# A hybrid MLA and sliding-window decoder step on one core: weight rings, the values' weights and the sums of squares between the two layers

## The reference

```python
for i in range(DEPTH):
    ap = rmsnorm(hp, pre_norm[i])
    ...
        mp = gated_out(o.reshape(n_b, seq, MLA_WIDTH), gate, mla_w_o[l])      # i = 0
        ...
        q, k, v, gate = swa_project(ap, swa_w_in[l])                          # i = 1
    ...
    hp = hp + rmsnorm(mp, post_norm[i])
```

## Time and profile before

| | |
|---|---|
| median of 3 runs | 1773.57 us (1772.23 to 1782.35) |
| the profiled execution | 1772.12 us |
| its span, first to last instruction | 1770.4 us |
| mean granted clock of TensorE | 0.963 |
| PE busy | 1628.7 us, 92% |
| DVE busy | 820.6 us, 46% |
| ACT busy | 545.9 us, 31% |
| POOL busy | 733.1 us, 41% |

### The profile page before, as it was taken

One profiled execution on the slowest core, in us unless ns is written; L12 is line 12 of the kernel. 1 busy time (PEld: TensorE's weight loads), 2 busy tenths in 40 slices (PEclk: granted clock), 3 DMA queues, 4 the chain that ended last, 5 costly groups with the idle time before them and its releaser, 6 DMA issues. The chain is left out here.

```text
span 1770.4 us, 28128 instructions
## 1 busy us (share of the span) xinstructions
PE 1628.7 (92%) x10778; PEld 1521.7 (86%) x10778; DVE 820.6 (46%) x1474; ACT 545.9 (31%) x1201; POOL 733.1 (41%) x891
## 2 busy tenths in 40 slices
PE   6999997899999999999988879997999899799797
PEld 6989997799989999998986569997899899576697
DVE  5127311676575766657563310038543201587016
ACT  5022111344444444444432210022222201576012
POOL 2323332255554555555445214545233222487410
PEclk9999998999999999999999989998999999799698
DMA  4112231111121111121149872252543122542214
GB/s 169 60 48 95 95 113 64 36 61 51 63 66 52 57 63 64 57 66 57 40 157 309 315 286 73 71 191 96 189 158 134 38 86 107 156 120 72 82 48 160
DMA packets 101406, 186.92 MB, mean 106 GB/s; under 512 B 11058, under 2 KB 65091, under 8 KB 100995
## 3 DMA queue, kind: packets, MB, share of 16 engines
q1 hardware_dynamic: 86628, 139.36, 23.6%
q0 software_dynamic: 8448, 24.65, 4.0%
q10 hardware_dynamic: 6208, 21.26, 3.0%
HBM read 137.42 MB, written 49.89 MB: 106 GB/s over the span
## 5 line engine op out<-in xcount | busy, mean ns | idle before, releaser
L607 POOL TENSOR_SCALAR b_prob<-b_prob,b_share 128x896 f32<-128x896 f32 (+7 forms) x128 | 97.1, 760 | 198.5 <-DVE b_share L806 196.7
L1607 POOL CAST w_hi_d<-w_raw_d 128x1024 fp32r<-128x1024 f32 x50 | 55.9, 1118 | 289.8 <-PE ps L129 114.7
L129 PE MATMUL ps<-a_xh,w_hi_a 128*128 128x344 f32 x552 | 119.6, 325 | 13.7 <-DVE a_xl L280 10.5
L707 ACT ACTIVATE b_pth<-ps 128x512 fp32r<-128x512 f32 (+1 forms) x160 | 86.2, 555 | 104.3 <-PE ps L930 94.7
L129 PE MATMUL ps<-a_xl,w_hi_a 128*128 128x344 f32 x552 | 118.2, 323 | 0.0
L129 PE MATMUL ps<-a_xh,w_lo_a 128*128 128x344 f32 x552 | 117.3, 321 | 0.0
L797 DVE TENSOR_REDUCE b_least<-ps 128x1 f32<-128x896 f32 (+7 forms) x128 | 96.3, 752 | 35.6 <-PE ps L916 34.9
L698 ACT ACTIVATE b_prob<-ps,b_least 128x896 f32<-128x896 f32 (+7 forms) x128 | 94.9, 744 | 57.1 <-DVE b_least L797 56.2
L811 DVE TENSOR_TENSOR b_ptl<-ps,b_pth 128x512 fp32r<-128x512 f32 (+1 forms) x160 | 99.2, 633 | 27.1 <-ACT b_pth L707 26.1
L1869 PE MATMUL ps<-xo_h,w_hi_d 128*128 128x344 f32 x352 | 98.3, 331 | 13.7 <-DVE w_lo_d L1747 7.1
L1610 POOL TENSOR_TENSOR w_lo_d<-w_raw_d,w_hi_d 128x1024 fp32r<-128x1024 f32 x42 | 106.2, 2529 | 3.4
(11 more groups left out here) (324 smaller groups left out, 4618.4 us busy)
## 6 DMA issues: line engine op xcount, KB each, us to landing
w_raw_d<-in_w_tiles SPq DMA_DIRECT2D x52, 512.0 KB, 3.6
c_pages<-in_cache_pages SPq DMA_DIRECT2D x80, 160.0 KB, 4.4
w_raw_a<-in_w_tiles SPq DMA_DIRECT2D x23, 512.0 KB, 3.5
gate_scratch<-a_stage ACTq DMA_DIRECT2D x16, 512.0 KB, 2.6
b_gate<-gate_scratch SPq DMA_DIRECT2D x64, 128.0 KB, 2.5
oh_scratch<-b_oh POOLq DMA_DIRECT2D x64, 128.0 KB, 2.1
ol_scratch<-b_ol POOLq DMA_DIRECT2D x64, 128.0 KB, 2.1
xo_h<-oh_scratch SPq DMA_DIRECT2D x16, 512.0 KB, 10.6
```

What stands on the lines that cost most here:

```text
L129: mm = nc.tensor.matmul(ps[:, bank + c, 0:CH], wt, xt[:, k0 + k, c * CH:(c + 1) * CH], start=first and x == 0, stop=last and x == 2)
L607: nc.gpsimd.tensor_scalar(prob[:, n % 4, 0:keys], prob[:, n % 4, 0:keys], share[:, n % 4:n % 4 + 1], 1.0, ALU.mult, ALU.mult).then_inc(nor ...
L707: nc.scalar.activation(pth[:, n % 4, 0:cols], ps[:, 4 + n % 2, 0:cols], ACT.Copy).then_inc(pt_hi, 1)
L1607: nc.gpsimd.tensor_copy(w.hi[:, t % 2, :], w.raw[:, t % 2, :]).then_inc(w.rounded, 1)
```

## The change

It edits only the stretch between the layers, `mla_samples` and `out_and_swa_front`.

- **Samples.** The products with `xo_l` of heads 0 to 7 now stand ahead of the transpose; those of heads 0 and 1 with `xo_h` follow; then tile 1's low part and heads 8 to 15 of `xo_l`. `LOW_PARTS` are four groups of four heads.
- **Raw ring.** Six tiles of the second pass (20, 21, 24, 25, 28, 29) are loaded into two more places, `raw_more`. So a load waits for the split of the tile four before; tiles 20 and 21 wait only for `totals`.
- **High and low ring.** In the second pass it has three places; the third is 8 blocks of 128 columns each for high and low inside `xo_l`, columns that the first pass has used. `parts`, `parts_of` and `shaped` give the views.
- **Values.** Tiles 42 and 43 have high and low places of their own, `wv_hi` and `wv_lo`, and wait for the stores of h (`h_out`). Tiles 44 and 45 follow the use of tiles 40 and 41 in the ring.
- **DVE's order.** The remainders of tiles 23, 25 and 27 stand ahead of a step each; the sums of the late squares 2 to 4 are spread anew. `sum_late`, `diag_early` and some other small tiles move; the late squares have three places instead of four.
- **Sums of h's late squares.** POOL adds squares 0 to 3 (three additions, behind the split of tile 33), DVE adds 4 to 7 (three) and then both sums (one).
- **PE.** The replication of the late inverse roots stands ahead of the product group k = 4 instead of behind it.
- **Sinks.** DVE negates them behind the first two queries.

The diff, cut to its core:

```diff
-LOW_PARTS = (range(0, 5), range(5, 9), range(9, 13), range(13, 16))
+LOW_PARTS = (range(0, 4), range(4, 8), range(8, 12), range(12, 16))
...
         mm.then_inc(cols_made, 1)
-        pe.wait_ge(w.split, 2)
-        part(1, range(KT), range(2), w.lo, g.xo_h)
+        low(0, False)
+        low(1, False)
         pe.wait_ge(cols_kept, 1)
...
         pe.wait_ge(xo_first_in, 32)
         part(0, range(2), range(2), w.hi, g.xo_h)
-        part(0, range(2), range(2), w.lo, g.xo_h)
-        for i, heads_in in enumerate(LOW_PARTS):
...
+        part(0, range(2), range(2), w.lo, g.xo_h).then_inc(w.used, 1)
+        pe.wait_ge(w.split, 2)
+        part(1, range(KT), range(2), w.lo, g.xo_h)
+        low(2, False)
+        low(3, True).then_inc(w.used, 1)
...
+    third = xo_l[:, 0:KT, CH:CH + P], xo_l[:, 0:KT, CH + P:CH + 2 * P]
+    raw_more = at("m_raw_more", [P, 2, D], 156672)
+    wv_hi, wv_lo = at("f_wv_hi", [P, 2, D], 200064, R32), at("f_wv_lo", [P, 2, D], 191808, R32)
...
+    v_tiles = (first_f + NQ + NKV - 2, first_f + NQ + NKV - 1)
+    raw_slot = [2 + t % 2 if t in (20, 21, 24, 25, 28, 29) else t % 2 for t in range(n_tiles)]
+    raw_before = [max((b for b in range(t) if raw_slot[b] == raw_slot[t]), default=None) for t in range(n_tiles)]
+    slot = [(t - N_OUT + 2) % 3 if N_OUT <= t < first_f else t % 2 for t in range(n_tiles)]
+    slot_before = [max((b for b in range(t) if slot[b] == slot[t] and b not in v_tiles), default=None) for t in range(n_tiles)]
...
-            split_done(sp, t - 2)
-            nc.sync.dma_start(w.raw[:, t % 2, :], a["w_tiles"][tile]).then_inc(w.landed[t % 2], 16)
+            sp.wait_ge(totals, 1) if raw_before[t] is None else split_done(sp, raw_before[t])
+            nc.sync.dma_start(raw_tile(t), a["w_tiles"][tile]).then_inc(landed[raw_slot[t]], 16)
...
+            if t in v_tiles:
+                pool.wait_ge(h_out, 32 * KT)
+            else:
+                pool.wait_ge(w.used, max((slot_before[t] or 0) + 1, N_OUT - 1 if slot[t] == 2 else 0))
...
+        for t in range(2, first_f + 2):
+            split(t)
+        for k in range(1, 4):
+            pool.wait_ge(h_sq, KT + k + 1)
...
+            nc.gpsimd.tensor_tensor(h_sum[:, SPLIT:TOK], h_sq_late[:, 0, :] if k == 1 else h_sum[:, SPLIT:TOK],
+                                    h_sq_late[:, k, :], ALU.add).then_inc(h_added_pool, 1)
+        for t in range(first_f + 2, n_tiles):
+            split(t)
...
-        for k in range(1, KT):
-            add_square(1, k)
+        for k in range(5, KT):
+            add_square_late(k)
+        dve.wait_ge(h_added, KT + 2)
+        dve.wait_ge(h_added_pool, 3)
+        nc.vector.tensor_tensor(h_sum[:, SPLIT:TOK], h_sum[:, SPLIT:TOK], h_sq_late[:, 4, :], ALU.add).then_inc(h_added, 1)
...
-                wh, wl = w.hi[:, half, k * P:(k + 1) * P], w.lo[:, half, k * P:(k + 1) * P]
+                wh, wl = parts_of(t, k)
...
-        for k in range(2, 5):
+        for k in range(2, 4):
             part(0, k, (0, 1))
         pe.wait_ge(spaced, 2)
         pe.wait_ge(unit, KT)
         replicate(diag_late, 0, 7)
+        part(0, 4, (0, 1))
         part(0, 5, (0, 1))
...
-                for x, (xt, wt) in enumerate(((g.xh, w.hi), (g.xh, w.lo), (g.xl, w.hi))):
+                for x, (xt, wt) in enumerate(((g.xh, wv_hi), (g.xh, wv_lo), (g.xl, wv_hi))):
```

More of the change, by code:

```diff
@@ L1423, in tensor, with low @@
         mm.then_inc(cols_made, 1)
-        pe.wait_ge(w.split, 2)
-        part(1, range(KT), range(2), w.lo, g.xo_h)
+        def low(i, last):
+            pe.wait_ge(xo_low_in[i], 16 * len(LOW_PARTS[i]))
+            for h in LOW_PARTS[i]:
+                mm = part(h // KT, range(h % KT, h % KT + 1), range(2), w.hi, xo_l, last=last and h == H - 1)
+            return mm
+        low(0, False)
+        low(1, False)
         pe.wait_ge(cols_kept, 1)
@@ L1782, in vector, with add_square_late @@
+        def add_square_late(k):
+            dve.wait_ge(h_sq, KT + k + 1)
+            if k > 5:
+                dve.wait_ge(h_added, KT + k - 6)
+            nc.vector.tensor_tensor(h_sq_late[:, 4, :], h_sq_late[:, 4, :], h_sq_late[:, k, :], ALU.add).then_inc(h_added, 1)
         for j in range(1, KT):
             add_early(j)
-        rest(N_OUT + 1)
+        rest(17)
         spaces(of_early, diag_early, 6, rooted, 1, inverted, spaced)
-        rest(N_OUT + 3)
+        rest(19)
         dve.wait_ge(replicated, 2)
@@ L1807, in vector @@
+        rest(27)
+        to_unit(0, 6), add_x(0, 6), x_low(0, 5), add_square(5), add_late(3)
+        to_unit(0, 7), add_x(0, 7), x_low(0, 6), add_square(6)
+        rest(29)
+        x_low(0, 7), add_square(7), add_late(4)
+        add_late(5)
+        rest(31)
+        add_late(6)
+        add_late(7)
         spaces(of_late, diag_late, 3, rooted, 2, inverted, spaced)
@@ L1810, in vector @@
         dve.wait_ge(read_late, KT)
[L1811 to L1812 removed]
+        to_unit(1, 0), add_x(1, 0)
         for k in range(1, KT):
@@ L1843, in vector @@
         scale(0), scale(1), query_low(0), query_low(1)
+        dve.wait_ge(sinks_in, 16)
+        nc.vector.tensor_scalar(g.nsinks[:], g.sinks[:], -1.0, None, ALU.mult).then_inc(negated, 1)
         for j in range(2, NQ):
```

104 lines of the change are left out of this document (52 added, 52 removed).

## The result

| | before | after |
|---|---|---|
| median | 1776.78 us (9 runs, 1772.23 to 1782.35) | 1767.28 us (9 runs, 1755.36 to 1769.46) |
| the profiled execution | 1772.12 us | 1767.28 us |
| its span | 1770.4 us | 1765.6 us |
| mean granted clock | 0.963 | 0.961 |

The ratio is 0.9926, with a 95% interval of 0.9907 to 0.9945: the change makes the kernel faster by 0.7%. That ratio stands for some 13 us; the two medians are 9.5 us apart. Forecast were 1747.5 us and a range of 1738 to 1758, which the measured time lies outside. The sign is right, but only about half of the 25.5 us came, and in the stages of the two profiles, as follows, only a third.

A forecast was written before the change was run, and what follows sets the result against it. PE, busy in 92% of the span, can gain only at waits and the slow clock behind them. Gains 0 + 5 + 8.4 + 6.6 + 5.5 = 25.5 us off 1772.1 give 1746.6, median 1748.1; stated 1747.5, range 1738 to 1758.

The forecast's parts named there:

- The samples: Samples' last products, up to tile 2: no gain, since tile 2 lands at the same time; bounds -1 to +2.6 us.
- The second pass: The pass of 16 tiles between the layers: 5 us sooner, with ends of 1 and 10 us.
- With the durations that DVE has now: Second pass: DVE's remainders and steps in their new order, timed with lengths from the trace before the change.
- The sum step by step: Second pass: adding DVE's and PE's times in order, the pass ends at 1245.6 instead of 1248.49, 2.9 us sooner.
- its first term: Second pass: DVE's remainder of tile 23, ahead of step 3, ends at 1198.6 + 1.2 = 1199.8 us.
- a deeper ring adds no DVE time: Second pass, 1183 to 1233 us: DVE is the bound there, and more ring places give it no extra time.
- The term on the side of the loads: Second pass: tile 22, loaded earlier, is ready at 1194.9 us, so PE's wait of 2.06 us before it goes.
- tile 28's bank: Second pass: PE waits 2.1 us before tile 28 until ACT has read bank 4, with 1.7 us for the clock.
- DVE sets the pace as before: Rival: the second pass gains nothing and POOL's adds take their full price; gain 17.1 us, to 1756.5; chance 0.14.
- the third place's shape: Rival: casts and remainders slow on the third place's 8 blocks of 128 columns, 34 us lost, 1787 us; chance 0.03.
- From the pass to the first job: Second pass's end to the first full job: 8.4 us sooner, with ends of 5 and 11 us.
- Values and gates: Value tiles and first gates: PE's waits of 3.74 and 3.83 us go with their clock, gaining 6.6 and 5.5 us.

The follow-up runs named there:

- e4: The changed kernel with POOL's eight remainders of the second pass cut to 8 of 1024 columns: 1751.91 us, pass 66.01 us.
- e1: The changed kernel run again, unedited: 1763.95 us, pass 77.63 us.
- e5: The changed kernel with all 16 remainders of the second pass on DVE, POOL keeping the casts: 1759.0 us, pass 73.95 us.
- e7: The changed kernel with all 16 second-pass remainders on DVE and POOL's split of tile 34 held behind the sum of h: 1754.24 us.
- e11: e7 with ACT reading the output of tiles 24 and 25 out of tile 28's bank before the last step's rounding: 1752.22 us.

## Why the prediction was half right

**The samples: right.** 0 was forecast and 0.2 us measured. The wait of 5.31 us turned into others of 3.40, 3.31 and 2.11, and tile 2's landing still sets the end.

**The second pass: wrong by 8.3 us (+3.3 on the mean, -5 forecast), sign included.** The failed step is "With the durations that DVE has now": the cost of DVE's own queue. I had called DVE the bound, read its durations from a trace in which POOL idles for loads, and kept them for a kernel whose whole point is that POOL idles no longer. The sum step by step reckoned DVE's order, not who shares its time. It fails at its first term: the remainder of tile 23 was to end at 1199.8, 26.6 us behind the early sums, and ended 30.4 behind them, so that PE waited 3.00 us before tile 23. The sentence "a deeper ring adds no DVE time" is refuted: DVE's operations were held up by 18.5 us instead of 13.4, and by 13.9 with two places and the same order. The term on the side of the loads came true: tile 22 was to be ready at 1194.9, 21.7 us behind the early sums, and was at 21.8. And the sum gave 2.9 us, not 5; the rest was put on it for the case that POOL holds DVE up less than before, and the opposite came. I even quoted the exclusion, but only behind the pass, where POOL's additions are new; for the pass I considered only that DVE might be held up less. By the Trainium skill (SBUF — State Buffer, "Who interferes with whom") the exclusion holds for the full instruction. The trace agrees: the sum at 1202.30 ends 0.37 us behind POOL's remainder of 1201.74, and takes 0.51 us in e4. The second wrong size is tile 28's bank: forecast as a wait of 2.1 us, measured 4.39, for the same reason, since ACT reads the bank behind the second operation of step 7, and ahead of that a low part took 3.08 us, an addition of squares 1.70 and that second operation 1.67. The rival "DVE sets the pace as before" came nearest in its mechanism, but it stopped at zero: a loss of the pass stood in no case but that of the third place's shape.

**From the pass to the first job: 2.8 of 8.4 us.** The step that failed is a place in time: the joining addition was to end at 1271.0, one microsecond ahead of POOL's remainder at 1272.0, and POOL's rounding of the same tile, which starts 1.3 us ahead of that remainder, was not in the sum. The addition came later than that. Replication did start DVE's chain 0.9 us sooner, but ACT's rounding of the second block then waited behind its copy of the replicated roots, DVE waited 1.32 us for it, and POOL's additions took 0.93 to 1.18 us each, not 0.8, and held three of DVE's operations. The last low part ended 1.1 us later than forecast, the rounding took 0.7 us more off the three additions, and so the joining one fell beside the remainder (2.54 us), PE waited 4.17 us, not 0.4, and its clock fell again to 0.50. A margin of one microsecond against a cost of 2.5 us and a clock stretch was no basis for one value. The sinks' negation, moved away, ends the wait for the sinks at 1284.76; the stretch from sums to job shrank by 1.8 to 3.1 us. How much of that is the sinks' was not tried apart from PE's new order there.

**Values and gates: the mechanism right, the size 9.0 instead of 12.1.** Both waits, 3.74 and 3.83 us, went. Of the clock, forecast at 4.6 us, and of the waits 3.1 did not come. First, 1.03 us of wait for ACT's copies is new among the values and 0.30 at the gate. Second, the wait for `s_q` grew from 9.63 to 10.90 us; but the next two waits for it shrank from 2.41 to 1.32, so 1.1 of these 1.3 us only lie behind the ledger's last border. Taken to the first product behind them (`ps<-ident,s_prob`), the gain of values and gates is 10.1 us. What is still missing was not found in a row, and may be the clock's.

**The chances.** Faster by over 1% had 0.80; measured were 0.7%, in the band called no change, which had 0.17. I had ranged the pass from 1 to 10 us and the stretch behind it from 5 to 11. Both came out below their low ends, because no end let POOL hold DVE up more than before.

What stays open: why the same wait costs clock in one execution and not in another, by which one code's pass scatters by 1.5 us (PE starts tile 28 61.2 and 61.0 us behind the early sums in after and in e1, each time 4.39 us late; in the 6.5 us behind it after has clock 0.52, e1 0.76) and by 2.4 between e5 and e7; how much of the 3.3 us is the high and low ring's third place and how much the raw ones' (they were not tried apart), and whether e11 differs from e7, whose intervals overlap.

## What to carry to other kernels

Where two engines hold each other up, as DVE and POOL do here, giving the one more buffers can slow the other: before deepening a ring, ask whether its filler holds up the engine that bounds the stretch, and price that engine's operations as if the filler never paused. Then it can pay to move work onto the busier engine: eight remainders of 1.2 us on DVE cost less than eight of 2.4 to 3.3 on POOL that hold it up. A single short operation on the critical path (here the last addition of a chain) deserves a wait on the other engine in front of it, which was worth some ten times the division of the work ahead of it (3.4 to 4.7 us against 0.35). And a weight ring that passes a stage of another form (the values in pairs) wants places of its own there: that edit gave 9 of its 12 us whatever stood beside it.
